# Prompt attention in a hybrid decoder step: four query tiles of a head share one product per tile of values, and gated heads go branch by branch

## What is computed

```
a     = exp(logsigmoid(z) + sum of later log_keep)       # stick-breaking, z = q k^T / sqrt(128), causal
o_sb  = a @ v
o_dsa = softmax(q k^T + bias, keys the indexer picked) @ v
o_cmp = softmax(q cmp_k^T + bias) @ cmp_v                # at most 16 summaries of 32 rows
o_slc = softmax(q slc_k^T + bias) @ slc_v
o_win = softmax(q win_k^T + bias) @ win_v
o_nsa = g0 * o_cmp + g1 * o_slc + g2 * o_win
y     = x + rmsnorm(concat(o_sb * silu, o_dsa * silu, o_nsa * silu) @ w_out)
```

## Time and profile before

| | |
|---|---|
| runs | 2479.27 us median of 3 (2478.28 to 2479.59) |
| the profiled execution | 2478.93 us, of which its span is 2477.2 us |
| PE busy | 2288.4 us (92%) |
| DVE busy | 937.6 us (38%) |
| ACT busy | 857.8 us (35%) |
| POOL busy | 507.6 us (20%) |
| mean granted TensorE clock | 0.96 of 2.4 GHz |

### The profile page before, as it was taken

One profiled execution on the slowest core, in us unless ns is written; L12 is line 12 of the kernel. 1 busy time (PEld: TensorE's weight loads), 2 busy tenths in 40 slices (PEclk: granted clock), 3 DMA queues, 4 the chain that ended last, 5 costly groups with the idle time before them and its releaser, 6 DMA issues. The chain is left out here.

```text
span 2477.2 us, 46126 instructions
## 1 busy us (share of the span) xinstructions
PE 2288.4 (92%) x16625; PEld 1747.2 (71%) x16625; DVE 937.6 (38%) x1657; ACT 857.8 (35%) x1913; POOL 507.6 (20%) x403
## 2 busy tenths in 40 slices
PE   5999999999999999997899999789799867998996
PEld 3887777767777676774899999555555544777885
DVE  4111121211121111124488886533333347975123
ACT  4000322222222222211444443355455466662010
POOL 6333222222222222221300000000000000445332
PEclk6999999999999999999999999899999876999998
DMA  4755676767667676657666664899999876002323
GB/s 150 209 173 199 230 253 208 263 214 251 236 223 247 229 253 223 205 136 218 188 194 196 194 195 147 249 369 377 319 382 377 294 229 198 1 1 94 120 85 119
DMA packets 322723, 523.15 MB, mean 211 GB/s; under 512 B 36981, under 2 KB 128518, under 8 KB 320662
## 3 DMA queue, kind: packets, MB, share of 16 engines
q1 hardware_dynamic: 302722, 491.76, 59.8%
q10 hardware_dynamic: 16416, 23.13, 2.8%
q0 software_dynamic: 3360, 5.33, 0.6%
HBM read 497.83 MB, written 44.00 MB: 219 GB/s over the span
## 5 line engine op out<-in xcount | busy, mean ns | idle before, releaser
L547 POOL TENSOR_TENSOR proj_w_lo<-kept_region,proj_w_hi 128x1024 fp32r<-128x1024 f32 (+1 forms) x120 | 282.1, 2352 | 743.1 <-DVE proj_w_hi L785 743.1
L565 PE MATMUL proj_acc<-proj_w_hi,h_hi 128*128 128x512 f32 (+1 forms) x960 | 395.0, 411 | 6.0 <-POOL proj_w_lo L547 6.0
L567 PE MATMUL proj_acc<-proj_w_lo,h_hi 128*128 128x512 f32 (+1 forms) x960 | 372.4, 388 | 0.0
L566 PE MATMUL proj_acc<-proj_w_hi,h_lo 128*128 128x512 f32 (+1 forms) x960 | 372.1, 388 | 0.0
L737 ACT COPY proj_kT<-proj_tp 128x512 f32<-128x512 f32 x256 | 150.4, 587 | 406.2 <-PE proj_tp L626 405.9
L565 PEld LDWEIGHTS proj_acc<-proj_w_hi,h_hi 128*128 128x128 f32 x960 | 180.9, 188 | 88.9 <-issue 53.5
L785 DVE CAST proj_w_hi<-kept_region 128x1024 fp32r<-128x1024 f32 (+1 forms) x120 | 86.8, 725 | 400.7 <-PE proj_acc L569 398.1
L567 PEld LDWEIGHTS proj_acc<-proj_w_lo,h_hi 128*128 128x128 f32 x960 | 180.8, 188 | 38.0
L566 PEld LDWEIGHTS proj_acc<-proj_w_hi,h_lo 128*128 128x128 f32 x960 | 181.6, 189 | 27.9
L1191 ACT COPY cmp_xT<-cmp_tp 128x512 f32<-128x512 f32 x260 | 139.3, 588 | 159.1 <-PE cmp_tp L1104 159.0
L626 PE MATMUL proj_tp<-kept_consts,kept_region 128*128 128x128 f32 x1024 | 153.6, 272 | 0.2 <-DMA kept_region<-in_cache_sb_kv_dram 0.2
(11 more groups left out here) (446 smaller groups left out, 3607.0 us busy)
## 6 DMA issues: line engine op xcount, KB each, us to landing
kept_region<-in_cache_sb_kv_dram SPq DMA_DIRECT2D x256, 256.0 KB, 4.9
kept_second<-in_cache_sb_kv_dram SPq DMA_DIRECT2D x256, 256.0 KB
kept_second<-in_cache_nsa_kv_dram SPq DMA_DIRECT2D x512, 128.0 KB, 2.4
kept_region<-in_w_in_dram SPq DMA_DIRECT2D x112, 512.0 KB, 5.8
kept_region<-in_cache_nsa_kv_dram SPq DMA_DIRECT2D x128, 256.0 KB, 5.0
kept_region<-in_cache_dsa_kv_dram SPq DMA_DIRECT2D x128, 256.0 KB, 4.8
kept_second<-in_cache_nsa_kv_dram SPq DMA_DIRECT2D x64, 256.0 KB, 4.8
kept_rows<-in_cache_nsa_kv_dram SPq DMA_DIRECT2D x64, 256.0 KB, 5.5
```

The costliest lines, as they stand in the source:

```text
L547: pool.tensor_tensor(w_lo[p % SPLIT][:, :, here], w[p % RAW][:, :, here], w_hi[p % SPLIT][:, :, here], ALU.subtract).then_inc(lo_made, 1)
L565: pe.matmul(to, h_hi[:, kk, r], hi[:, k], start=first, stop=False)
L566: pe.matmul(to, h_lo[:, kk, r], hi[:, k], start=False, stop=False)
L567: last = pe.matmul(to, h_hi[:, kk, r], lo[:, k], start=False, stop=final)
```

## The change

All 22 runs of four units with wide products (4 stick, 6 slc, 6 win, 6 dsa; a run is the four query tiles of one branch of one head) now write their transposed probabilities into one buffer of 128 x 4 x 512 (key block, query), and the product is done once, with the unit of tile 3: four matmuls, key block j against the queries of tiles j to 3, so 512, 384, 256 and 128 columns wide. Before it were ten of 128 columns. PE waits for all four copies ahead of them. There are two such buffers (WB = 2): a new one, and the second half of `kept.second`, so only two of the three pieces of output weights are loaded early (OUT_EARLY = 2); the third is loaded at the start of `finish`. A cmp unit keeps a product of its own, from a small buffer that lies in the `soft` tiles. The gated units are reordered: a head's four slc units, then its four win, then its four cmp.

```diff
@@ -2347,7 +2347,9 @@
     for h in range(6):
         for i in range(4):
             units.append(Unit("slc", 10 + h, i, 10 + h, 6 + h // 3, 6 + h // 3, 6 + h, 6 + h, True, False))
+        for i in range(4):
             units.append(Unit("win", 10 + h, i, 10 + h, 8 + h // 3, 8 + h // 3, 6 + h, 12 + h, False, False))
+        for i in range(4):
             units.append(Unit("cmp", 10 + h, i, 10 + h, h // 3, h // 3, 6 + h, h, False, True))
...
+    WB = 2
+    runs = [x for x in units if x.kind != "cmp" and x.tile == 3]
+    run_of = {x.u: sum(y.u < x.u for y in runs) for x in units}
+    products = [x for x in units if x.kind == "cmp" or x.tile == 3]
+    product_after = {x.u: sum(y.u <= x.u for y in products) for x in units}
...
-        pT = [s.sb(f"pT{i}", [P, 4, P]) for i in range(TB)]
-        nmax, sums, rcp = s.sb("nmax", [P, N]), s.sb("sums", [P, N]), s.sb("rcp", [P, N])
+        pT = [s.sb("pT", [P, 4, SEQ])[:], kept.second[:, OUT_EARLY * OUT_KP * CH:].rearrange("p (j t) -> p j t", t=SEQ)]
+        pT_few = [t[0:16, 0:P] for t in softs]
+        nmax, sums, rcp = s.sb("nmax", [P, N])[:], s.sb("sums", [P, N])[:], pT[0][:, 1, 0:N]
...
-            for n in range(OUT_RAW):
+            for n in range(OUT_EARLY):
                 out_load(sp, io, kept, n)
...
             def product(x):
-                wait_copied(pe, x.u)
-                if x.u == 0:
+                if x.kind != "cmp" and x.tile < 3:
+                    return
+                if x.kind == "cmp":
+                    wait_copied(pe, x.u)
+                    pe.matmul(ov[place[x.out] % 2][:, x.tile, :], kept.cmp_vp[0:x.blocks, x.v, :], pT_few[small_place[x.u] % 2][0:x.blocks, :],
+                              start=False, stop=True, skip_group_check=True).then_inc(multiplied, 1)
+                    return
+                for u in range(x.u - 3, x.u + 1):
+                    wait_copied(pe, u)
+                if x.u == 3:
                     pe.wait_ge(kept.v_in, 16 * 4)
...
-                to = ov[place[x.out] % 2][:, x.tile, :]
-                if x.kind == "cmp":
...
-                else:
-                    for j in range(x.tile + 1):
-                        last = pe.matmul(to, kept.v[:, j, x.v * DH:(x.v + 1) * DH], pT[x.u % TB][:, j, :],
-                                         start=(x.first and j == 0), stop=(x.last and j == x.tile), skip_group_check=True)
+                to = ov[place[x.out] % 2][:].rearrange("p m t -> p (m t)")
+                for j in range(4):
+                    last = pe.matmul(to[:, j * P:], kept.v[:, j, x.v * DH:(x.v + 1) * DH], pT[run_of[x.u] % WB][:, j, j * P:],
+                                     start=(x.first and j == 0), stop=(x.last and j == 3), skip_group_check=True)
                 last.then_inc(multiplied, 1)
...
         def copy(eng, x):
...
-            do(pT[x.u % TB][0:rows, 0:n, :], tp[x.u % TB][0:rows, 0:n, :]).then_inc(copied[by_act[x.u]], 1)
+            run, n = run_of[x.u], x.tile + 1
+            if run >= WB:
+                eng.wait_ge(multiplied, product_after[runs[run - WB].u])
+            do(pT[run % WB][:, 0:n, x.tile * P:n * P], tp[x.u % TB][:, 0:n, :]).then_inc(copied[by_act[x.u]], 1)
...
-OUT_RAW, OUT_KP = 3, 2
+OUT_RAW, OUT_KP, OUT_EARLY = 3, 2, 2
...
             for n, (c, e) in enumerate(pieces):
                 if n >= RAW:
                     sp.wait_ge(lo_made, n - RAW + 1)
+                if n >= OUT_EARLY:
                     out_load(sp, io, kept, n)
```

More of the change, by code:

```diff
@@ L2365, in prompt_attention @@
     TURN, MUL = 3, 5
+    WB = 2
[3 more added lines that the diff above has]
+    product_after = {x.u: sum(y.u <= x.u for y in products) for x in units}
+    small = [x.u for x in units if x.kind == "cmp"]
+    small_place = {u: n for n, u in enumerate(small)}
     with ExitStack() as ctx:
@@ L2385, in prompt_attention @@
         ops_until = lambda u: min(n_ops, (u + 1) * n_ops // (n_free - 4))
-        by_act = [u % 2 if u < n_stick else int(u % 3 > 0) for u in range(N)]
+        by_act = [x.u % 2 if x.kind == "stick" else int(x.kind in ("slc", "win")) if x.kind != "dsa" else int(x.u % 3 > 0) for x in units]
         def wait_copied(eng, u):
@@ L2455, in product @@
             def product(x):
-                wait_copied(pe, x.u)
-                if x.u == 0:
+                if x.kind != "cmp" and x.tile < 3:
[8 more added lines that the diff above has]
+                if x.u == 3:
                     pe.wait_ge(kept.v_in, 16 * 4)
-                if x.tile == 0 and x.first and place[x.out] >= 2:
+                if x.first and place[x.out] >= 2:
                     pe.wait_ge(out_done, place[x.out] - 1)
-                to = ov[place[x.out] % 2][:, x.tile, :]
-                if x.kind == "cmp":
-                    last = pe.matmul(to, kept.cmp_vp[0:x.blocks, x.v, :], pT[x.u % TB][0:x.blocks, 0, :], start=False, stop=True, skip_group_check=True)
-                else:
-                    for j in range(x.tile + 1):
-                        last = pe.matmul(to, kept.v[:, j, x.v * DH:(x.v + 1) * DH], pT[x.u % TB][:, j, :],
-                                         start=(x.first and j == 0), stop=(x.last and j == x.tile), skip_group_check=True)
+                to = ov[place[x.out] % 2][:].rearrange("p m t -> p (m t)")
+                for j in range(4):
+                    last = pe.matmul(to[:, j * P:], kept.v[:, j, x.v * DH:(x.v + 1) * DH], pT[run_of[x.u] % WB][:, j, j * P:],
+                                     start=(x.first and j == 0), stop=(x.last and j == 3), skip_group_check=True)
                 last.then_inc(multiplied, 1)
@@ L2481, in copy @@
             eng.wait_ge(turned, x.u + 1)
-            if x.u >= TB:
-                eng.wait_ge(multiplied, x.u - TB + 1)
             do = eng.copy if by_act[x.u] else eng.tensor_copy
-            n = 1 if x.kind == "cmp" else x.tile + 1
-            rows = x.blocks if x.kind == "cmp" else P
-            do(pT[x.u % TB][0:rows, 0:n, :], tp[x.u % TB][0:rows, 0:n, :]).then_inc(copied[by_act[x.u]], 1)
+            if x.kind == "cmp":
+                if small_place[x.u] >= 2:
+                    eng.wait_ge(multiplied, product_after[small[small_place[x.u] - 2]])
+                do(pT_few[small_place[x.u] % 2][0:x.blocks, :], tp[x.u % TB][0:x.blocks, 0, :]).then_inc(copied[by_act[x.u]], 1)
+                return
+            run, n = run_of[x.u], x.tile + 1
+            if run >= WB:
+                eng.wait_ge(multiplied, product_after[runs[run - WB].u])
+            do(pT[run % WB][:, 0:n, x.tile * P:n * P], tp[x.u % TB][:, 0:n, :]).then_inc(copied[by_act[x.u]], 1)
         @block.gpsimd
@@ L2588, in invert @@
                     cm = kept.pmask[:, C_CM - C_PM:C_CM - C_PM + x.blocks]
-                    dve.wait_ge(small, chain.step(dve.scalar_tensor_tensor(v, v, 1.0, cm, ALU.mult, ALU.mult, accum_out=sums[:, x.u:x.u + 1])))
+                    dve.wait_ge(small_step, chain.step(dve.scalar_tensor_tensor(v, v, 1.0, cm, ALU.mult, ALU.mult, accum_out=sums[:, x.u:x.u + 1])))
                 total = sums[:, x.u:x.u + 1]
                 if x.kind == "cmp" and x.tile == 0:
-                    dve.wait_ge(small, chain.step(dve.tensor_scalar(r, total, 1e-30, None, ALU.max)))
+                    dve.wait_ge(small_step, chain.step(dve.tensor_scalar(r, total, 1e-30, None, ALU.max)))
                     total = r
```

7 lines of the change are left out of this document (4 added, 3 removed).

## The result

The changed kernel takes 2499.77 us (median of 4 runs, 2492.51 to 2503.3) against 2479.43 (4 runs, 2478.28 to 2481.04) in the same comparison: a ratio of 1.008, 95% interval 1.0064 to 1.0097. It is slower by about 20 us, of which the profiled execution shows 13.6: that one ran in 2492.51 us, with a span of 2490.7.

What follows compares the result with a forecast made beforehand. With PE and DVE both near full in the gated stretch, their mutual waits count: 14.2 us new idle less 6.2 and 1.3 gives +6.7; plus stick 0, DSA 0.6, stage end 0.2: +7.5, 2486.8 us, range 2478.5 to 2493.5.

Steps and rivals of the forecast that it cites:

- loop A: Gated heads, first cmp step: the slc run's product delays the next score, DVE idles 1.1 us, 6 times, 6.6 us.
- loop B: Next head's first slc step: the win run's product delays the next score, DVE idles 1.3 us, 5 times, 6.5 us.
- The first win step: Start of the gated stretch: the last stick run's product falls there and costs about 1.1 us of DVE idle time.
- the 6.2 us of waits for scores: Gated stretch: DVE's waits for scores, 6.2 us over six heads, vanish whole because other steps have no product.
- The exponentials: Gated stretch: of DVE's 6.4 us of waits for exponentials, 1.3 go through the new unit order.
- DSA heads: DSA stretch: +0.6 us, from late copies (+1.0) less cheaper wide products (0.4); end of the stage, +0.2 us.
- rival 2: Stick stretch: two or three of four products at 1.2 GHz add 3 us to the forecast, 2490 us; chance 0.15.
- width: All 22 runs: wide matmuls gain 0.07 us a run, 1.5 us in all, 0.4 us where PE sets the pace.
- the third piece of output weights: `finish`: loading this piece later costs 0; at most a load, 3.7 us, if its cover were gone.
- rival 4: Product starts: loads were not hidden, so 66 fewer starts save 7.9 us, 2471 us; chance 0.04.
- rival 3: Gated stretch: DVE's queue of work covers the lump, so only the savings count, 2471 us; chance 0.06.
- Rival 1: Gated loops: smaller bubbles, half of 14.2 us, net about 0 to +3, 2481 us, within 0.2%; chance 0.3.

Runs made afterwards that it cites:

- the repeat: The changed kernel run once more, unedited: 2497.97 us (5 runs), ratio 1.0077, stage 194.6 us.
- experiment 6: The changed kernel plus one filler matmul of 512 columns per gated head, ahead of the transposes of win tile 1: 2497.18 us, ratio 1.0074.
- experiment 9: The changed kernel with products spread over four steps and four small buffers, without key blocks 1 and 2 of win runs: 2478.03 us, stage 172.7.
- experiment 1: The kernel before with only the new order of gated units, each unit keeping its own product: 2475.69 us, ratio 0.9988.
- experiment 3: The changed kernel with a run's four wide matmuls spread over four steps, gate multiplication three steps later: 2481.61 us, ratio 1.0014.
- experiment 4: The changed kernel with a run's product still at one go, but as ten matmuls of 128 columns: 2501.98 us, ratio 1.0094.
- 11: The kernel before with only the new order of gated units, the sum's start set with the head's first tile alone: 2476.35 us, ratio 0.9994.

## Why the prediction was wrong

The direction and the mechanism held: slower, by the lumps of the product in two loops between PE and DVE. The size didn't: +20 us by the medians, +15.9 by the stage, where I had +7.5, and the measured time lies 6 us above my range.

- **The loops were sized about right.** Loops A and B came to 1.1 and 1.3, 2.4 us a head. Over the three middle heads `add` waits 3.2 us in A, 1.1 a head, and 4.4 in B (1.66, 1.54 and 1.16), 1.5 a head. The first win step cost 1.6 instead of 1.1.
- **The step that failed is the credit: "the 6.2 us of waits for scores, which I take to vanish whole".** The sum was read from a group over all of 2116.5 to 2207.5 and taken for six alike heads. They aren't alike. These are `add`'s waits for PE by gated head, added up from both timelines (us):

| gated head | 1 | 2 | 3 | 4 | 5 | 6 | all |
|---|---|---|---|---|---|---|---|
| before | 0.34 | 0.55 | 0.67 | 0.92 | 0.21 | 5.63 | 8.3 |
| after | 3.07 | 2.48 | 3.22 | 2.84 | 4.21 | 6.38 | 22.2 |
| after, outside the lumps' stops | 0.45 | 0 | 0.57 | 0.37 | 0 | 2.22 | 3.6 |

  Two thirds of the waits of before lie in the last head, where PE already does the scores of the DSA units and is the bound (DVE's timeline, the kernel before):

```profile
2204.16 0.42 DVE L2578 CUSTOM_DVE_ANT_0 pa_logits<-pa_sc,kept_bias 128x256 f32<-128x256 f32 x1 [1.30 <-PE pa_sc L2434]
...
2205.92 0.56 DVE L2578 CUSTOM_DVE_ANT_0 pa_logits<-pa_sc,kept_bias 128x384 f32<-128x384 f32 x1 [1.26 <-PE pa_tp L2449]
...
2208.00 0.69 DVE L2578 CUSTOM_DVE_ANT_0 pa_logits<-pa_sc,kept_bias 128x512 f32<-128x512 f32 x1 [1.26 <-PE pa_tp L2452]
```

  There PE's work stays, and so do waits: 2.2 us are left besides the lumps' stops, and the sixth lump of win products, for which I had put nothing because it falls into the DSA stretch, brings a stop of 2.5. So of the 8.3 us only 4.7 went, and with that stop set against them 2.2, where I had credited 6.2. The exponentials gave a little more than I took: 6.4 before, 4.5 after, 1.9 instead of 1.3. A middle head is then 2.5 + 0.3 - 0.7 - 0.2 = 1.9 longer (loops, rest, and the two credits); the table of the stage has 1.7, 1.8 and 2.0, where I named 1.0 to 1.2.
- **The gated part in all**, first win step included, is 13.3 us longer where I had 6.7. Of the 6.6 that I missed, the credit for scores is 4.0, the clock fall 1.4, loop A without that fall 1.3 (7.9 for 6.6), the first win step 0.5 and loop B 0.2, less the 0.6 for exponentials. This adds up to 6.8.
- **DSA heads: +2.5 instead of +0.6 and +0.2.** I had a late copy of 0.25 us in four heads, 1.0. PE's waits there are for the last copy of a run (2220 to 2257.5, the changed kernel), 1.9 us where the kernel before has 0.3:

```profile
PE pa_ov L2483 <- DVE kept_second L2508: 1.0, 1, 1.0
PE pa_ov L2483 <- ACT pa_pT L2508: 0.6, 2, 0.3
PE pa_ov L2483 <- ACT kept_second L2508: 0.3, 1, 0.3
```

  The three of 0.3 us are the late copies, and their size was right. The other is a copy on DVE, in the last unit, which PE awaits for 0.98 us; the last piece is 0.6 us longer, the bound that I had named and then cut to 0.2. The rest is no wait: behind the last gated head's multiplication PE's records make 32.0 us where they made 31.3, although the wide products should save 0.4. So PE has more left to do when that multiplication comes; why, no run here shows.
- **Half clock** (rival 2, 0.15) is real, but I placed it in the stick stretch alone. There it costs 3.1 us when it comes, the 3 that I had; it came in the repeat and not in the first profile. In the gated heads I had none, and one in each profile of the change costs about 1.5. It follows a lull that is the loop's wait on PE's side; with that lull filled (experiment 6) the profile has no such fall.
- **Right**: width worth 0.07 us a run, stick heads unchanged where the clock held, `finish` and the third piece of output weights at no cost (234.1 us against 234.2), no exposed loads (rival 4), DVE's queue doesn't cover the lump (rival 3). Rival 1 fell: the bubbles weren't smaller.

By stage time the account is: before 175.7; new order alone 173.1; run's product of four matmuls spread over four steps 179.2 (the slc steps too full for PE, experiment 9); the same in one lump 191.6 to 194.6; narrow in one lump 197.9, with one clock fall more.

**What stays open.** The medians of the change lie 4 to 7 us above its fastest, profiled runs, and those of the kernel before up to 6.7 above its fastest. Half clock in the stick stretch is some of it. Some may lie ahead of the stage, where all these kernels are the same: its first score comes between 2061.7 and 2071.1 us in the fourteen profiles, which is why the sizes above go by the stage. For experiments 1 and 3 I had expected runs within 3 us of each other; they spread over 8.7 and 9.3, though no gated head of theirs has a clock fall in the profile. What makes the part ahead of the stage vary no run here settles. Nor was the change tried with PE's work moved so that the wide product falls into the win steps.

## What to carry to other kernels

Two engines that feed each other in a fixed order meet at every step, not on average: joining four products into one leaves every total as it is, and each thing queued behind it (the next score, a small copy's buffer) waits for all of it. Count work by section of the cycle, put what the other engine needs first ahead of the long piece, and check each buffer count against the new distance between write and release. Before you credit a wait that a group shows, find in the timeline where it lies: a wait at the seam between two stretches can't be taken off the heads in the middle.

## What the runs showed of the hardware that I had not expected

- A burst of matmuls behind a short lull ran at the lower clock level: eight records in 3.66 us instead of 2.23, at a granted clock of 0.60, after 1.35 and 0.46 us without work and two transposes between them. In the repeat the same lull left the product at 2.23, and a shorter one (1.14 and 0.46) was followed by the lower level, 0.62.
- A product of 4 to 16 rows of values against 128 columns takes 0.41 us to the next operation (2144.11 to 2144.53 in the changed kernel's timeline of PE), about twice a full one (0.22). There are four such in a gated head, and three of them stand in the section where PE is the bound.
- Where each slc tile's product started a sum of its own on its 128 columns, the output lacked part of the head's sum (experiments 1 and 4, by the same amount); with the start on the head's first tile alone and all else equal it didn't (11). So a start reaches beyond the columns that the matmul writes: later products into the other columns of the same `ov` tile began anew instead of adding.
